# A gathered weighted sum: for 23 of 256 rows, half of the sum on VectorE beside TensorE

## What is computed

```python
# per token: 8 heads, 16 chosen experts per head, out of 16384
act = gelu(einsum('thkd,td->thk', u[expert], xt))        # a dot of 1024 with row u
return einsum('thk,thkd->td', w * act, v[expert])        # weighted sum of the rows v
```

## Time and profile before

| | |
|---|---|
| runs | 1101.57 us median of 3 (1101.25 to 1103.44) |
| the profiled execution | 1103.55 us, span 1101.8 us |
| mean granted TensorE clock | 0.983 of full speed |
| busy share of the span | PE 92%, DVE 58%, ACT 41%, POOL 29% |
| read from HBM | 345.25 MB, of it 269.89 MB on the queue of the gathers |

### The profile page before, as it was taken

One profiled execution on the slowest core, in us unless ns is written; L12 is line 12 of the kernel. 1 busy time (PEld: TensorE's weight loads), 2 busy tenths in 40 slices (PEclk: granted clock), 3 DMA queues, 4 the chain that ended last, 5 costly groups with the idle time before them and its releaser, 6 DMA issues.

```text
span 1101.8 us, 10631 instructions
## 1 busy us (share of the span) xinstructions
PE 1016.8 (92%) x3544; PEld 566.9 (51%) x3544; DVE 642.9 (58%) x1495; ACT 454.7 (41%) x1168; POOL 314.1 (29%) x307
## 2 busy tenths in 40 slices
PE   8999999999999999999999898998898988877778
PEld 8887458544686466554454343554433432322224
DVE  2515265305343479877776676766558668667443
ACT  1133244311264138545544544345344354344333
POOL 3000000001000023445635353453434344443430
PEclk9999999999999999999999898999899999999999
DMA  8435433244625459999999999999999999999990
GB/s 317 153 132 229 153 104 126 77 153 172 229 87 229 172 209 421 402 398 419 421 421 421 422 420 422 420 421 421 421 421 421 421 421 416 421 422 422 420 402 28
DMA packets 46679, 347.26 MB, mean 315 GB/s; under 512 B 5056, under 2 KB 6464, under 8 KB 9120
## 3 DMA queue, kind: packets, MB, share of 16 engines
q0 software_dynamic: 37584, 269.89, 59.3%
q1 hardware_dynamic: 9040, 76.69, 18.4%
HBM read 345.25 MB, written 1.05 MB: 314 GB/s over the span
## 4 chain that ended last, share of the span: by engine, by line
PE 58%; DMA 30%; ACT 6%; DVE 5%; issue 2%; POOL 0%; POOLq 0%; DVEq 0%
DMA tail<-in_peer_uv,small 15%; PE pp L1122 15%; DMA xc_rg<-in_peer_uv,small 8%; PE pp L649 8%; PE pp L677 5%; PE pp L673 4%; PE pp L659 3%; DMA ig<-in_peer_uv,small 3%; PE pp L804 3%; PE pp L782 2%; PE pp L824 2%; DMA spare<-in_peer_uv,small 2%; PE pp L1014 2%; PE pp L1218 2%; PE pa L1079 1%
## 5 line engine op out<-in xcount | busy, mean ns | idle before, releaser
L1565 ACT ACTIVATE small<-small 128x1 f32<-128x1 f32 x256 | 51.5, 201 | 308.2 <-DVE small L2273 306.6
L1579 ACT ACTIVATE diag<-ident,small 128x128 f32<-128x128 f32 x256 | 102.8, 402 | 9.7 <-PE pp L1122 1.4
L649 PE MATMUL pp<-hT,ring 128*128 128x256 f32 x384 | 83.4, 379 | 0.8 <-DVE hT L1714 0.8
L1122 PE MATMUL pp<-xc_rg,diag 128*128 128x512 f32 x128 | 66.1, 641 | 18.1 <-ACT diag L1579 17.9
L1571 ACT ACTIVATE small<-small 128x1 f32<-128x1 f32 x256 | 75.4, 294 | 9.3
L649 PEld LDWEIGHTS pp<-hT,ring 128*128 128x128 f32 x384 | 72.9, 190 | 10.8 <-issue 1.0
L1122 PE MATMUL pp<-sm,diag 128*128 128x512 f32 x128 | 64.1, 625 | 12.4 <-ACT diag L1579 12.3
L1122 PE MATMUL pp<-tail,diag 128*128 128x512 f32 x128 | 62.4, 610 | 10.9 <-ACT diag L1579 10.9
L1122 PE MATMUL pp<-kT,diag 128*128 128x512 f32 x128 | 63.1, 616 | 9.5 <-ACT diag L1579 9.5
L1122 PE MATMUL pp<-ig,diag 128*128 128x512 f32 x128 | 64.6, 629 | 7.6 <-ACT diag L1579 6.5
L1122 PE MATMUL pp<-spare,diag 128*128 128x512 f32 x128 | 63.7, 621 | 8.5 <-ACT diag L1579 8.5
(11 more groups left out here) (489 smaller groups left out, 1905.6 us busy)
## 6 DMA issues: line engine op xcount, KB each, us to landing
ring<-in_wall SPq DMA_DIRECT2D x31, 2048.0 KB, 7.7
ring<-in_wall SPq DMA_DIRECT2D x4, 512.0 KB, 7.2
ring<-in_wall SPq DMA_DIRECT2D x1, 1280.0 KB
xs<-in_x SPq DMA_DIRECT2D x2, 512.0 KB, 3.8
post_g<-in_rows POOLq DMA_DIRECT2D x2, 512.0 KB, 8.2
tail<-in_wall SPq DMA_DIRECT2D x1, 1024.0 KB, 11.1
kT<-in_wall SPq DMA_DIRECT2D x1, 1024.0 KB, 13.1
lt<-in_sub_keys SPq DMA_DIRECT2D x1, 1024.0 KB, 7.4
```

The lines of the kernel that those rows point to most:

```text
L649: ins = nc.tensor.matmul(buf[:, c, :], mine, h3[:, k, :], start=(k == 0), stop=(k == KC - 1))
L1122: ins = nc.tensor.matmul(acc[t][:, c, :], diag[:, n * P:(n + 1) * P], rows_uv[page_of(g)][:, D + c * HALF:D + (c + 1) * HALF], start=False ...
L1565: nc.scalar.activation(acts[:, at:at + BATCH], dots[:, at:at + BATCH], ACT.Gelu_apprx_tanh)\
L1579: nc.scalar.activation(diag[:, n * P:(n + 1) * P], ident[:, :], ACT.Copy, scale=wk[:, g % LAG:g % LAG + 1]).then_inc(s["diag_made"], 1)
```

## The change

For the 23 slots in `HALVES` (every third from 36 to 102) PE multiplies only the first 512 columns of the row v. The other 512 are weighed and added up by DVE, in place in SBUF, four slots later (`HALF_LAG`), after the dot and the choice steps of slot g + 4. POOL's gather into a place that held such a slot waits for DVE's part too (`row_weighed`). At slot `TILE_SLOTS` + 4 DVE adds its sum to the residual, ahead of the addition that was there. Two semaphores that nobody waits for (`v_blocks_made`, `co_used`) are dropped from the list and from the instructions that signalled them; these signal `dve_step` in place of them, and wait for themselves as before.

```diff
+HALVES = list(range(36, 105, 3))
+HALF_LAG = 4
...
                 if slot_before(g) is not None:
                     pool.wait_ge(s["row_used"], slot_before(g) + 1)
+                if slot_before(g) in HALVES:
+                    pool.wait_ge(s["row_weighed"], HALVES.index(slot_before(g)) + 1)
...
-                for c in range(2):
+                for c in range(1 if g in HALVES else 2):
                     ins = nc.tensor.matmul(acc[t][:, c, :], diag[:, n * P:(n + 1) * P],
...
+            half_sum = xs[:, D:D + HALF]
+
+            def half_weighed(g):
+                dve.wait_ge(s["w_made"], g + 1)
+                row, weight = rows_uv[page_of(g)][:, D + HALF:2 * D], wk[:, g % LAG:g % LAG + 1]
+                if g == HALVES[0]:
+                    dve.wait_ge(s["row_used"], g)
+                    ins = V.tensor_scalar(half_sum, row, weight, None, ALU.mult)
+                else:
+                    dve.wait_ge(s["row_weighed"], HALVES.index(g))
+                    ins = V.scalar_tensor_tensor(out=half_sum, in0=row, scalar=weight, in1=half_sum, op0=ALU.mult, op1=ALU.add)
+                ins.then_inc(s["row_weighed"], 1)
...
                 dot(g)
                 for _ in range(choice_rate(g)):
                     next(between, None)
+                if g - HALF_LAG in HALVES:
+                    half_weighed(g - HALF_LAG)
                 if g == 1:
                     att_biased(2)
...
                 if g == TILE_SLOTS + 4:
+                    dve.wait_ge(s["row_weighed"], len(HALVES))
+                    step(V.tensor_tensor(x3[:, 0, HALF:D], x3[:, 0, HALF:D], half_sum, ALU.add))
                     dve.wait_ge(s["row_used"], TILE_SLOTS)
```

More of the change, by code:

```diff
@@ L117 @@
         "o_std", "nsa_sums", "nsa_std", "nsa_scaled", "nsa_turned", "nsa_normed", "cmp_in", "cmp_shifted", "hid_made",
-        "cmp_full", "cmp_sums", "cmp_std", "cmp_ready", "v_blocks_made", "cmp_turned", "cmpT_made", "cs_full", "cs_shifted",
-        "cs_exp", "cs_ready", "cs_turned", "csT_moved", "co_full", "co_used", "att_full", "att_bias", "att_exp",
+        "cmp_full", "cmp_sums", "cmp_std", "cmp_ready", "cmp_turned", "cmpT_made", "cs_full", "cs_shifted",
+        "cs_exp", "cs_ready", "cs_turned", "csT_moved", "co_full", "att_full", "att_bias", "att_exp",
         "att_turned", "att_moved", "ao_full", "ao_used", "nsa_osums", "nsa_ostd", "nsa_out", "mix_turned",
@@ L123 @@
         "choice_step", "top_shift", "top_exp", "chosen", "prob_made", "dot_made", "gelu_made", "w_made", "diag_made",
-        "row_used", "half_summed", "h2_made", "gate_full", "gate_moved", "y_made"]
+        "row_used", "row_weighed", "half_summed", "h2_made", "gate_full", "gate_moved", "y_made"]
 UPDATE_BANKS = (0, 1, 2)
@@ L2002, in _ @@
                                  vc_psum.unsqueeze(1).broadcast_to([P, NSA_HEADS, DH]),
-                                 head_mask.unsqueeze(2).broadcast_to([P, NSA_HEADS, DH]), ALU.mult), "v_blocks_made")
+                                 head_mask.unsqueeze(2).broadcast_to([P, NSA_HEADS, DH]), ALU.mult))
             dve.wait_ge(s["cmp_std"], 1)
@@ L2096, in _ @@
             step(V.tensor_tensor(at2.no[:, HALF:2 * HALF].rearrange("p (m n) -> p m n", n=DH),
-                                 co_psum[:, HALF:2 * HALF].rearrange("p (m n) -> p m n", n=DH), heads_of(1), ALU.mult),
-                 "co_used")
+                                 co_psum[:, HALF:2 * HALF].rearrange("p (m n) -> p m n", n=DH), heads_of(1), ALU.mult))
             mixed_gained(1, 0, 4, pa[:, D:D + HALF])
```

## The result

The changed kernel takes 1113.63 us, the median of 4 runs (1110.93 to 1114.38), beside 1101.51 us before (1101.25 to 1103.44, 4 runs): a ratio of 1.0103 with a 95% interval of 1.009 to 1.0115. The two medians lie 12.1 us apart (1.0110), the ratio over the single runs stands for 11.3 us; in the text I use the medians. The forecast was slower by 4.7 us. The profiled execution took 1114.38 us, with a span of 1112.6.

A forecast was written before the change was run, and what follows sets the result against it. DMA bytes were taken to bound the kernel at 421 GB/s. 0 for PE, 0 for DVE's work and + 4.7 us for late gathers on 1101.57 gave 1106.3 us, with a range of 1100.6 to 1115.

The forecast's parts named there:

- PE's 19.8 us: PE loses 0.86 us in each of 23 slots, between some 503 and 690 us; costed at nothing, since transfers cover it.
- DVE's work hides, 16.6 us at nothing: DVE's 24 added operations at 0.69 us make 16.6 us, hidden in its 61.6 us idle in 500 to 705 us.
- The new wait makes gathers late: POOL's gather for slot g + 8 also waits for DVE, behind the dot of g + 4; at slot 60, 6.6 us later.
- The size of the covers: Time from a gather's issue to the landing of the row ahead: 3.0 to 5.3 us over the 23 slots, but for four.
- The price of a short cover, 0.25 us each, 4.7 us in all: Loss per gather issued with little DMA work ahead: 2.7/11 = 0.25 us from 450 to 478 us; times 19, 4.7 us.
- my 19 short covers: The 23 slots less four near SP's weight loads; each gather issued 3.0 to 5.3 us before the row ahead lands.
- My upper bound: At most some 0.75 us for each of 19 late gathers, from 2.9 us over slots 22 to 25: 14.3 us.
- Deep enough: Rival: the DMA queue is deep enough for the later gathers, so nothing is lost; 1101.6 us, chance 0.33.
- Starved each time: Rival: every late gather starves the engines, the queue never recovers until slot 110; 0.75 us each, 1116 us, chance 0.15.
- PE is what matters: Rival: relieving PE from slot 36 on, where its bound stretch ends, makes the kernel faster; 1101.1 us, chance 0.05.
- the 412 GB/s named: Sign: in 500 to 705 us the DMA rate should fall to some 412 GB/s (4.7 of 205 us).
- gathers of 1.5 us and over: Sign: POOL gathers this long, stretched by starting within a DVE dot, should be more frequent in the changed kernel.

The follow-up runs named there:

- PE's part alone: Changed kernel without DVE's weighing, final addition and POOL's new wait; PE takes one product in the 23 slots, the second half is left out: 1102.19 us, ratio 0.9999.
- the work alone: Changed kernel, but DVE does its 23 operations on a fixed tensor in place of the row and POOL doesn't wait for them: 1102.32 us, ratio 0.9999.
- the wait without the work: Changed kernel, but PE takes both products again and DVE does a one-column operation that POOL still waits for; no final addition: 1111.22 us, ratio 1.0075.
- a late wait on PE alone: Kernel before, but POOL's gather into the place of one of the 23 slots waits until PE has used the row four slots later: 1134.71 us, ratio 1.0286.
- the lag of five: Changed kernel, with DVE weighing five slots later and not four: 1142.13 us, ratio 1.0357.
- PE's wait of three slots: Kernel before, but POOL's gather into the place of one of the 23 slots waits until PE has used the row three slots later: 1116.47 us, ratio 1.0120.

## Why the prediction was right or wrong

- **Bytes bound the kernel; PE's 19.8 us are worth nothing.** Right. PE's part alone measures 0.9999 of before. The term of 0.86 us per slot was right, but not the 19.8 us of busy time: with half of the products gone PE was busy for 12.6 us less in 500 to 705 us (172.84 and 185.47). The granted clock of that stretch was 0.94 in place of 0.97; at full speed, by my estimate from these numbers, it is some 17 us less (172.84 x 0.94 and 185.47 x 0.97).
- **DVE's work hides, 16.6 us at nothing.** Right, and the work alone measures 0.9999. The operation took 0.73 to 0.75 us and not 0.69.
- **The new wait makes gathers late, and that is what costs.** Right, and shown from both sides: the wait without the work costs 9.1 us, the work without the wait nothing, and a late wait on PE alone 32.7.
- **The size of the covers.** The release was put too early, and the covers so too long, by two terms. POOL starts 0.77 us behind DVE's operation and not 0.3. That half microsecond also puts its start behind the start of the next dot in slots in which I had it ahead. I saw that a gather within a dot runs for up to 1.9 us, and named 0.9 us of cover for it, but then compared covers from the start of the instruction, in which this isn't contained.
- **The price of a short cover, 0.25 us each, 4.7 us in all.** This is the step that failed. The change costs 12.1 us, 12.1/19 = 0.64 us for each of my 19 short covers and 0.9 for each of the 13 that the trace shows below the limit. I had spread the loss of 2.7 us evenly over eleven gathers issued in 450 to 478 us. In that trace one row lost all of it, slot 24. It was one of two short covers whose instruction was also stretched (slots 23 and 24, 1.87 and 1.73 us): they end 2.9 and 3.0 us ahead of the landing before, where slot 22, just before, ended 4.0 us ahead and lost nothing. So the mean was taken over gathers of both kinds, while the changed kernel puts 11 of its 23 under 3.3 us. But of the two such gathers in the trace of before, slot 23 lost 0.1 us and slot 24 2.9, so that trace couldn't have given the price either. My upper bound, 0.75 us each and 1115.9 us, came close, but by luck: it spread 2.9 us over slots 22 to 25, and slot 25 had 7.5 us of cover (465.96 to 473.45) and not one of the least; 2.9/4 is 0.73.
- **The rivals.** "Deep enough" has fallen for four slots and is true for three. An estimate of 4.4 us for a single DMA of 1 MB follows from the Trainium skill, DMA: Bandwidth & Descriptors, "Anatomy of one DMA — SWDGE (gpsimd) path". Among other gathers it doesn't hold: slot 50 was issued at 533.38, 4.65 us ahead of its old landing (4.9 by my sum), and landed 9.1 us behind its issue. The shortest times that the traces with late gathers show are 4.4 us too, but from the end of POOL's instruction (in the lag of five and in PE's wait of three slots), so with the instruction itself some 5.4 us. "Starved each time" came nearer in time, but not every short cover starves the engines: 9 of the 23 gathers land more than 0.25 us late, and from slot 114 on the covers are 10 us and more again. "PE is what matters" has fallen, also where PE was the bound.
- **The signs to look for.** The rate fell further than the 412 GB/s named, to 391, and POOL waits for DVE, as named. Two signs did not come as named: gathers of 1.5 us and over became fewer in 500 to 705 us, 13 of 72 after 18 of 80, and PE lost 11.8 us of busy time. Waits of VectorE for a DMA by 3 us or more went only from 2 to 3 in that stretch, those by 1.5 us or more from 6 to 11.

## What to carry to other kernels

Where transfers bound a kernel, as here, taking work off a busy engine was worth nothing, and what decided on the change was how early each transfer was issued. A buffer that is freed by one more engine is freed by the later of the two, and an operation put behind a wait for a later transfer ties the refill to that transfer: with eight places and four slots of lag that cost 12 us, with three slots, or ahead of that wait, nothing that can be told from no change. A price for such a loss shouldn't be read from a mean over a stretch that holds long and short covers. Each short case should be looked at for itself, and where there are only two and they differ (0.1 and 2.9 us), what they give is a range and not a price.

## What of the hardware was not expected

- POOL started 0.77 to 0.80 us behind the end of a DVE operation that released it (20 releases in the changed kernel), and 0.26 us behind a matmul that did, whose end is modelled in the profile.
- Row 50 of the changed kernel landed 7.9 us behind the end of its gather instruction (534.56 to 542.47), though a row moves in 2.49 us and the rows ahead had landed by 536.62. In the runs with late gathers the landing of such a row came from 4.4 to 10.0 us behind the end of its instruction. What the engines do in that time stays open, as does whether the end or some point within POOL's instruction is what counts.
